# Expert up weights issued from ScalarE's DMA queue instead of SyncE's

## The reference, cut to what matters

```python
hg = jnp.einsum('sd,edf->sef', t, w_gate)
hu = jnp.einsum('sd,edf->sef', t, w_up)
act = jax.nn.silu(hg) * hu * combine[:, :, None]
return jnp.einsum('sef,efd->sd', act, w_down)
```

## Time and profile before

| | us |
|---|---|
| median of 3 runs (lowest, highest) | 684.89 (683.55, 685.63) |
| the profiled execution's own time | 686.04 |
| its span from first to last instruction | 684.3 |

### The profile page before, as it was taken

The page is one execution under the profiler, slowest core; times in us unless marked ns, Lnnn a source line. Parts: engine busy times, 40 slices in busy tenths (PEclk is TensorE's granted clock), DMA queues, the critical chain, the costliest instruction groups (busy, mean ns, idle before and its releaser), DMA issues.

```text
span 684.3 us, 11449 instructions
## 1 busy us (share of the span) xinstructions
PE 628.0 (92%) x4226; PEld 378.8 (55%) x4226; DVE 358.6 (52%) x869; ACT 179.4 (26%) x370; POOL 62.3 (9%) x111
## 2 busy tenths in 40 slices
PE   2799999998999999999998989999999999999894
PEld 1597758446766455545554457666555544555442
DVE  2257988998454643344334465735444344433445
ACT  2123252013431222122212233342223122221213
POOL 5010408950000000000000000000000000000000
PEclk9899999999999999999999999999999999999998
DMA  8999967999999999999999999999999999999991
GB/s 326 367 399 394 381 249 269 400 417 417 383 410 418 422 420 422 421 423 422 423 421 421 408 399 411 420 420 422 421 420 420 422 421 421 422 421 423 422 375 65
DMA packets 51534, 269.63 MB, mean 394 GB/s; under 512 B 4112, under 2 KB 6224, under 8 KB 27440
## 3 DMA queue, kind: packets, MB, share of 16 engines
q1 hardware_dynamic: 50720, 268.22, 96.6%
q0 software_dynamic: 784, 1.01, 0.5%
HBM read 268.17 MB, written 1.05 MB: 393 GB/s over the span
## 4 chain that ended last, share of the span: by engine, by line
PE 75%; DMA 17%; DVE 5%; issue 1%; SPq 0%; ACT 0%; POOL 0%; DVEq 0%; POOLq 0%
PE bank L983 15%; PE bank L995 14%; PE bank L1016 12%; DMA ring<-in_w_gate 11%; PE bank L1042 7%; DMA ring<-in_w_mod 6%; PE bank L860 4%; PE bank L699 4%; PE bank L948 2%; PE bank L783 2%; PE bank L793 2%; DVE hT L1781 2%; PE bank L612 2%; PE bank L1003 1%; PE bank L729 1%
## 5 line engine op out<-in xcount | busy, mean ns | idle before, releaser
L983 PE MATMUL bank<-ring,arena 128*64 128x256 f32 x1024 | 116.9, 380 | 3.5 <-DMA ring<-in_w_gate 3.5
L995 PE MATMUL bank<-ring,arena 128*64 128x256 f32 x1024 | 117.2, 381 | 0.0
L983 PEld LDWEIGHTS bank<-ring,arena 128*64 128x64 f32 x1024 | 75.6, 137 | 51.8 <-issue 21.6
L995 PEld LDWEIGHTS bank<-ring,arena 128*64 128x64 f32 x1024 | 72.3, 137 | 41.1 <-issue 8.6
L1781 DVE SCALAR_TENSOR_TENSOR hT<-hT,bank 128x256 f32<-128x256 f32 x32 | 19.2, 602 | 136.6 <-PE bank L995 136.6
L1310 ACT CAST xn_parts<-arena 128x512 fp32r<-128x512 f32 x64 | 39.6, 619 | 106.8 <-DVE arena L1806 106.8
L1806 DVE SCALAR_TENSOR_TENSOR arena<-bank,hT,gates 128x512 f32<-128x512 f32 x64 | 48.0, 750 | 36.7 <-PE bank L1016 35.4
L1042 PE MATMUL bank<-xn_parts,sel 128*128 128x512 f32 x256 | 67.1, 405 | 0.0
L1016 PE MATMUL bank<-dn_w,hT 128*64 128x512 f32 x256 | 58.5, 598 | 1.1 <-ACT gates L1120 1.1
L1042 PEld LDWEIGHTS bank<-xn_parts,sel 128*128 128x128 f32 x256 | 45.7, 188 | 20.9 <-issue 12.4
L1016 PE MATMUL bank<-xn,arena 128*64 128x512 f32 x112 | 51.1, 598 | 0.0
(11 more groups left out here) (326 smaller groups left out, 768.0 us busy)
## 6 DMA issues: line engine op xcount, KB each, us to landing
ring<-in_w_gate SPq DMA_DIRECT2D x32, 2048.0 KB, 18.3
ring<-in_w_up SPq DMA_DIRECT2D x32, 2048.0 KB, 18.8
ring<-in_w_mod SPq DMA_DIRECT2D x20, 2048.0 KB, 17.5
dn_w<-in_w_down SPq DMA_DIRECT2D x16, 2048.0 KB, 18.3
xn<-in_w_down SPq DMA_DIRECT2D x14, 1024.0 KB, 16.9
gates<-in_w_down SPq DMA_DIRECT2D x14, 1024.0 KB, 19.8
ring<-in_w_in SPq DMA_DIRECT2D x2, 2048.0 KB, 22.0
dn_w<-in_w_mod SPq DMA_DIRECT2D x2, 2048.0 KB, 12.0
```

The lines of the kernel that those rows point to most:

```text
L983: ins = pe.matmul(bank[2][h * WIN:(h + 1) * WIN, 0:FE], xw[:, b, h, k, :], w[:, h, 0, k, :], start=(k == 0), stop=(k == KT - 1))
L995: ins = pe.matmul(bank[3][h * WIN:(h + 1) * WIN, 0:FE], xw[:, b, h, k, :], w[:, h, 1, k, :], start=(k == 0), stop=(k == KT - 1))
```

## The change

For pairs 2 to 15 of both layers the up weights are issued by ScalarE, right behind the window copies of the same pair and ahead of the tanh of the pair before it; pairs 0 and 1 stay on SP. SP keeps gate and down loads, in their old order and with their old waits. ScalarE reads the pair's expert number from `eid_i` with a register load, and for that waits once per layer for the constants. There is no new wait for the ring: the wait for the up matmuls of pair p - 2 is the one that `window` already has. The last group on ScalarE is taken out of the loop and written out, so that no load is issued beyond the last pair.

```diff
--- before.py
+++ after.py
@@ -404,24 +404,17 @@
                     sp.wait_ge(E[l]["gate_done"], p - 1)
                     gate_load(l, b, e)
 
-                def up_next(p, b, e):
-
-                    sp.wait_ge(E[l]["unit_done"], p - 1)
-                    up_load(l, b, e)
-
-                gate_next(2, 0, 4), up_next(2, 0, 4), gate_next(3, 1, 6), up_next(3, 1, 6)
+                gate_next(2, 0, 4), gate_next(3, 1, 6)
                 sp.wait_ge(E[l]["down_done"], 2)
                 down(l, 4)
                 with sp.Fori(2, groups) as i:
                     e = expert_at(i * XS)
                     gate_next(i * 2, 0, e)
-                    up_next(i * 2, 0, e)
                     e = expert_at(i * XS - 2)
                     sp.wait_ge(E[l]["down_done"], i * 4 - 4)
                     down_second(l, e)
                     e = expert_at(i * XS + 2)
                     gate_next(i * 2 + 1, 1, e)
-                    up_next(i * 2 + 1, 1, e)
                     e = expert_at(i * XS)
                     sp.wait_ge(E[l]["down_done"], i * 4 - 2)
                     down(l, e)
@@ -1290,6 +1283,12 @@
                         ins = act.copy(xw[:, b, h], xgT[:, :, bass.ds(start, WIN)])
                     ins.then_inc(e["xw_ready"], 1)
 
+                def up_load(p, b):
+
+                    pair = act.value_load(eid_i[0:1, bass.ds(p * 2, 1)], min_val=0, max_val=NE - 2)
+                    act.dma_start(of_pair(ring_w, l, b)[:, :, 1], w_up[l][bass.ds(pair, 2)].rearrange("o (p k) f -> p o (k f)", k=KT)
+                                  ).then_inc(up_in[l][b], 16)
+
                 def tanh(p):
                     act.wait_ge(e["gate_done"], p + 1)
                     if not isinstance(p, int) or p >= 1:
@@ -1309,11 +1308,13 @@
                         act.wait_ge(e["y_kept"], p * 2 + (n + 1))
                         act.copy(xn_parts[:, 0, b, at], y_s[:, b, at]).then_inc(e["y_hi"], 1)
 
-                def group(i):
+                def group(i, last=False):
                     for b in range(2):
                         p = i * 2 + b
                         n = p if isinstance(i, int) else XS
                         window(p + 1, 1 - b)
+                        if not (last and b == 1) and n >= 1:
+                            up_load(p + 1, 1 - b)
                         tanh(p)
                         if n == 0 and l == 0:
                             keep_column((1, 4))
@@ -1343,10 +1344,12 @@
                         ins = act.copy(xw[:, 0, h, at], xgT[:, at, bass.ds(starts[h], WIN)])
                     ins.then_inc(ready, 1)
                 groups = act.value_load(grp_i[0:1, l:l + 1], min_val=0, max_val=(PASSES - 1) * NE // XS) + NE // XS
+                act.wait_ge(S["consts"], 2)
                 group(0)
                 group(1)
-                with act.Fori(2, groups) as i:
+                with act.Fori(2, groups - 1) as i:
                     group(i)
+                group(groups - 1, last=True)
                 high_y(groups * 2 - 1, 1)
 
             route(0)
```

## The result

The changed kernel takes 699.0 us (median of 4 runs, 697.89 to 700.23) against 684.5 us before (4 runs beside them). The ratio is 1.0196, with a 95% interval from 1.0171 to 1.0220: 13.4 us slower, between 11.7 and 15.1 (the two medians by themselves differ by 14.5). The forecast was 698.9. The profiled execution took 699.99 us, its span is 698.2.

A forecast was written before the change was run, and what follows sets the result against it. TensorE and DMA were both taken as full, with TensorE meeting the loads at each layer's end. Layer 0's 3.6 + 5.0, less 1.7, plus layer 1's 2.1 + 5.0 gave 14.0 us: 698.9 from 684.89, range 689 to 703.

The forecast's parts named there:

- rival "faster": Two queues fill the DMA engines better; needs a rate 2.9% higher, 433 GB/s; say 681 us, chance 0.07.
- (a): SP loses 28 up issues of some 0.38 us, but no gate or down goes earlier; worth 0.
- (b): ScalarE's added register load and issue, 0.7 us per pair before tanh, are covered by VectorE's 4.86 us wait; worth 0.
- (d): At both layer starts late up issues empty the queues; 3.6 us DMA time lost in layer 0, 2.1 in layer 1.
- rival "part of the price only": Order costs nothing, only idle time at the layer starts is left: 4.0 us, 688.9; range 687 to 696, chance 0.18.
- (e): At each layer's end, ups in their own queue make the last gate land one load later: 5.0 us per layer.
- The half share: With both queues full, the engines alternate between them, so each queue gets half of the bandwidth.
- The sum: Starts and order, less a 1.7 us mod wait, make the last gate 14.0 us late; 698.9 us, chance 0.64.
- a bound: Lower bound for the order at layer end: served in issue order, up 15 makes TensorE wait some 4.4 us.
- (c): In steady state ups are issued 8 us later, land 12.7 us after issue, 3 us early; cost 0.
- The waits move to the up matmuls: Listed sign that the forecast is wrong: TensorE would wait for loads at the up matmuls.
- The gate wait: TensorE's wait for loads at the gate matmuls was to grow from 3.5 to 19.2 us.

The follow-up runs named there:

- run 9: Against the old kernel: only the up loads of pairs 2 to 7 of each layer on ScalarE's queue, issued early; 686.28 us, ratio 1.0006.
- run 2: Against the changed kernel: the up load of pair 15 of each layer back on SP, behind gate 15; 695.46 us, ratio 1.0158.
- run 4: Against the old kernel: all ups still on SP's one queue, but issued as late as ScalarE issued them in the changed kernel; 698.62 us, ratio 1.0204.
- run 11: Against the old kernel: one queue, only the ups of pairs 2 to 7 of each layer issued late; 691.88 us, ratio 1.0087.
- run 3: Against the changed kernel: ups of pairs 2, 3 and 15 back on SP, pairs 4 to 14 on ScalarE; 692.9 us, ratio 1.0105.
- run 5: Against the changed kernel: the 28 ups stay on ScalarE's queue but are issued early, soon after the up matmuls; 693.63 us, ratio 1.0119.
- run 10: Against the old kernel: only the ups of pairs 8 to 15 of each layer on ScalarE's queue, issued early; 692.37 us, ratio 1.0106.
- run 6: Against the old kernel: the gate loads of pairs 2 to 15 on ScalarE's queue, ups and downs on SP; 692.56 us, ratio 1.0094.
- run 7: Against the old kernel: the down loads of pairs 2 to 14 on ScalarE's queue, gates and ups on SP; 695.81 us, ratio 1.0158.

## Why the prediction was right, and where it was off

**The bound held.** DMA share 1.01 and 421 to 422 GB/s in all full stretches, before and after. With it the rival "faster" fell: the rate did not rise by any of the 2.9% that it needed. The mechanism forecast, idle transfer time at the starts plus later gates, is what the runs show. That the total came so close (14.0 forecast, 13.4 measured, 14.0 in the profile) is in part luck: the terms for the starts were too low, those for the order too high, and 1.15 of the profile's 14.0 is not the change's.

**(a) and (b), costed at nothing.** Issues on ScalarE take 0.38 to 0.43 us; run 9, with 12 loads moved, differs from before by 0.4 us with an interval that holds 0. For all 28 it was not tried alone.

**(d) The starts.** Mechanism right, sizes low. Lost in layer 0: 4.8 us against 3.6, of which a part belongs to the late start of this execution. Runs 2, 4 and 11 issue up 2 and up 3 as late and began no later than the kernel before; their rates from 183 to 215 us, 361, 358 and 359 GB/s against 414, make it 4.0 to 4.3. By itself the late start of the layers cost 6.0 us (run 11), where the rival "part of the price only" had 3.6 - 1.7 + 2.1 = 4.0. One error in that sum shows in the waits: the 1.7 us that TensorE spent on a mod load between the layers were taken off, but with only the starts late this load is as late as the last gate, and the wait stays. In run 11, from 376 to 470 us:

```profile
PE bank L622 <- DMA ring<-in_w_mod: 1.8, 1, 1.8
```

Without that deduction the sum is 5.7. After the result I took the gap to belong to pairs 2 and 3; run 3 shows it at the first late load, whichever it is.

**(e) The order.** Here the sum for it alone is 5.0 - 1.7 + 5.0 = 8.3, and run 5, which has the second queue with issues only some 2 us late, measured 8.2 (6.2 to 10.0). Runs 9 and 10 put it in the last pairs. In the changed kernel itself the order cost less than the 5.0 us per layer of the sum. Gate 15 of layer 0 landed at 387.7 (363.58 + 24.1), 8.1 us later, with at least 4.8 of them lost at the start: about 3 for the order. The last gate of layer 1 is 14.0 later, the loads as a whole 9.7: about 4. The half share is in the trace. Of the changed kernel from 296 to 302 us, while both queues were full (packets, MB, share of 16 engines):

```profile
q10 hardware_dynamic: 156, 1.28, 51.1%
q1 hardware_dynamic: 157, 1.26, 50.4%
```

That is 213 and 210 GB/s. The Trainium skill's round-robin rule (DMA: Bandwidth & Descriptors, "Queues, rings and completion order") agrees with that. The Trainium skill's other rule, that issuing from several engines saves only the sequencer's time (same page, "Issuing engines are not separate DMA queues"), holds for the rate and not for the time of this kernel: by it alone run 5 would have been 685.7, and it was 693.6.

**The sum.** Two of its steps were added as if independent. The four cases say how far that goes (us over before; each of the three is known to within 2 us):

| | early issue | late issue |
|---|---|---|
| one queue | 0 | 14.0 (run 4) |
| two queues | 8.2 (run 5) | 13.4 (the change) |

Given two queues, lateness adds 5.2 us, near the 3.6 + 2.1 = 5.7 of my sum. Given late issue, the second queue adds nothing measurable: it delays the gates but brings the late ups forward. I had this as a bound, 4.4 us for a layer in one queue against 5.0 in two. So the 14.0 us of the sum came out (last gate 14.0 us later, layer 1's first gate matmuls at 456.04 against 449.26 before, 6.8 us for the 6.9 forecast; without the 1.15 us these are 12.8 and 5.6), but "starts plus order" is one way to split it. From the old kernel, late issue alone costs as much as the whole change.

**(c) was wrong in part.** Ups were to land 12.7 us after issue, 3 us early. The median is 14.1, and up 3 of each layer took 15.2 and 15.4 us and was late: in layer 0, gate 4 was issued 0.6 us behind it (205.06) and shared the engines. "The waits move to the up matmuls" was one of the signs of being wrong; it came true for these two loads and no other. TensorE, timeline of pair 3:

```profile
219.72 5.36 PE L988 MATMUL bank<-ring,arena 128*64 128x256 f32 x32 [2.10 <-DMA ring<-in_w_up]
225.01 1.20 PE L1035 MATMUL bank<-xn_parts,sel 128*128 128x512 f32 x4
```

**The gate wait** was forecast at 19.2 us and is 8.9. Part of TensorE's delay came under other names: 1.15 us before the experts began, 4.1 us at the two up 3, and 3.7 us of slower matmuls, nearly all behind up 3 of layer 0 and behind gate 10 of layer 1. When the last gates then came late, TensorE was late already. The step that failed is the one that put every us of delay on one line.

## What to carry to other kernels

A single queue in the order of use is a schedule: in this kernel the loads were served in the order in which they are needed. Moving one kind of load to a second queue gave it half of the engines (213 of 423 GB/s) and took the lead from the rest. That was free while the rest had lead to spare (run 9), and cost 6 to 11 us in all where compute had caught up with the loads (runs 5, 6, 7, 10). Before moving an issue, look at two things: when the new engine reaches it, beside the work that it does in between, and whether the DMA engines have anything left to do until then; here, bound by transfers, a gap of a few us at the start of a layer was still there at its end.

## What the runs showed that was not expected

A short wait of TensorE can cost more than itself, but need not. In the changed kernel five of its waits for expert weights lasted 2.0 to 2.4 us. Behind up 3 of layer 0 (2.10 us, shown above) the 32 matmuls took 5.36 us, where they take 3.5 to 3.7 otherwise, and so they did behind gate 10 of layer 1 (2.03). Behind the other three (2.03, 2.05 and 2.35 us) they took 3.67. One of either kind, both from layer 1:

```profile
497.95 3.67 PE L988 MATMUL bank<-ring,arena 128*64 128x256 f32 x32 [2.05 <-DMA ring<-in_w_up]
...
592.86 5.36 PE L976 MATMUL bank<-ring,arena 128*64 128x256 f32 x32 [2.03 <-DMA ring<-in_w_gate]
```

The granted clock from 220 to 225 us was 0.66, and from 593 to 598 as well:

```profile
220.00:225.00 5.00, 5.00 (x32) 2.80 (x28) 0.00 (x0) 0.00 (x0) 0.00 (x0) 0.66 1.02 424
593.00:598.00 5.00, 5.00 (x32) 3.50 (x30) 0.01 (x1) 0.88 (x2) 0.00 (x0) 0.66 1.01 419
```

It was 1.00 in both stretches before. So for a part of each the clock was at the lower of its two levels, 1.2 GHz, and TensorE had stood still for 2.0 to 2.1 us just ahead. What sets these two waits apart from the other three is not shown. The two slow groups make 3.5 of the 3.7 us by which the gate and up matmuls are busier than before (118.8 + 119.0 against the 116.9 of the earlier trace rows and the 117.2 of this line of the page before):

```profile
L995 PE MATMUL bank<-ring,arena 128*64 128x256 f32 x1024 | 117.2, 381 | 0.0
```

Waits of 0.8 us at the gates, as in run 5, left the busy time of the gate matmuls at 117.3. The clock is not what the change costs: the three other executions of the changed kernel had a mean granted clock of 0.990 to 0.991, against 0.983 in the profiled one and 0.991 in the profile of the kernel before, and still took 697.89 to 700.23 us.
